# A two-block transformer kernel on one Trainium2 core: the order of attention pairs, the place of the neighbourhood bias, and three small reorderings

## The reference

```python
# first block
sh1, sc1, g1, sh2, sc2, g2 = split(silu(c) @ w_mod + b_mod)           # modulation
proj = modulate(rmsnorm(x), sh1, sc1) @ w_in                          # the same for 256 context tokens
q_m  = rmsnorm(q_lat) @ w_uq      ;  kn, v_m = rmsnorm(kv_lat) @ w_ukv
o_mla = dense_attention(q_m + rope, [k_ctx, k], [v_ctx, v])           # 8 latent heads, 512 keys
s = q_na @ k_na * scale + bias[h]; s = where(col_in, s, -1e30)        # 8 neighbourhood heads,
o_na = softmax([s, s_ctx]) @ [v, v_ctx]                               # 256 own + 256 context keys
x = x + g1 * (concat(o_mla, o_na) @ w_out)
x = x + g2 * hierarchical_moe(...)                                    # 16 experts, 2 per token in one group
# second block
u, v, q, k, v_b, f = rmsnorm(x) @ w_in2
x = x + concat(spatial_gating(u, v), forgetting_attention(q, k, v_b, f)) @ w_out2
x = x + conv_ffn(rmsnorm(x))
return rmsnorm(x)
```

## Time and profile before

| what | value |
|---|---|
| three runs | 744.06, 744.93, 747.24 us |
| median | 744.93 us |
| profiled execution | 743.41 us |
| its span in the trace | 741.6 us |
| granted TensorE clock, mean | 0.999 |
| TensorE / VectorE / ScalarE / GpSimd busy | 96% / 61% / 45% / 10% |
| moved from HBM | 197.9 MB, 268 GB/s over the span |

### The profile page before, as it was taken

How to read it: one execution, slowest core, us unless ns; L and a number is a source line. 1 busy time by engine, 2 the same in 40 slices (tenths; PEclk the granted TensorE clock), 3 DMA queues, 4 the chain that set the end, 5 groups by cost and what they waited for, 6 DMA issues and landing times.

```text
span 741.6 us, 10899 instructions
## 1 busy us (share of the span) xinstructions
PE 715.0 (96%) x4132; PEld 500.7 (68%) x4132; DVE 449.6 (61%) x776; ACT 332.3 (45%) x583; POOL 76.8 (10%) x83
## 2 busy tenths in 40 slices
PE   8899998999999999999999999999999999999997
PEld 3597887655785344353354357878889888888885
DVE  1597897799555211221221148969768999998443
ACT  2475233687524001110110137746547777776433
POOL 0000001043000000000000000040001344444000
PEclk9999999999999999999999999999999999999999
DMA  9995987625278999999999999006306446495101
GB/s 371 408 380 237 363 353 271 214 100 227 82 274 339 388 425 427 425 420 427 428 430 420 421 425 391 38 1 234 137 1 227 151 190 226 154 413 226 57 1 57
DMA packets 21258, 199.50 MB, mean 269 GB/s; under 512 B 2368, under 2 KB 2880, under 8 KB 4832
## 3 DMA queue, kind: packets, MB, share of 16 engines
q1 hardware_dynamic: 20304, 195.35, 65.5%
q0 software_dynamic: 624, 3.28, 1.3%
q10 hardware_dynamic: 288, 0.30, 0.1%
HBM read 197.86 MB, written 1.05 MB: 268 GB/s over the span
## 4 chain that ended last, share of the span: by engine, by line
PE 71%; DVE 13%; DMA 10%; ACT 3%; issue 1%; POOL 1%; SPq 0%; DVEq 0%; POOLq 0%; ACTq 0%
PE banks L1801 13%; PE banks L2074 10%; PE banks L2116 8%; PE banks L1339 6%; PE banks L1838 6%; DMA ring<-in_w_up 5%; PE banks L2078 5%; DVE ring L2308 3%; PE banks L1756 2%; DMA ring<-in_w_mod 2%; DMA ring<-in_w_col 2%; PE banks L1584 2%; PE banks L1585 2%; PE banks L1586 2%; DVE w_lo L2165 2%; DVE nmax L2360 2%
## 5 line engine op out<-in xcount | busy, mean ns | idle before, releaser
L2165 DVE TENSOR_TENSOR w_lo<-ring,w_hi 128x1024 fp32r<-128x1024 f32 (+1 forms) x123 | 147.5, 1204 | 48.1 <-ACT w_hi L1197 24.1
L1801 PE MATMUL banks<-ring,att 128*64 128x512 f32 x448 | 113.3, 593 | 2.4 <-DMA ring<-in_w_up 2.4
L2074 PE MATMUL banks<-h_both,w_hi 128*128 128x512 f32 x320 | 80.1, 392 | 0.0
L1801 PEld LDWEIGHTS banks<-ring,att 128*64 128x64 f32 x448 | 38.5, 137 | 59.7 <-issue 53.4
L888 ACT ACTIVATE w_hi<-ring 128x1024 fp32r<-128x1024 f32 x50 | 51.9, 1052 | 29.1 <-PE banks L1339 18.1
L2074 PEld LDWEIGHTS banks<-h_both,w_hi 128*128 128x128 f32 x320 | 57.6, 189 | 10.3
L2580 DVE TENSOR_TENSOR front<-front,banks 128x512 f32<-128x512 f32 x8 | 5.5, 688 | 95.4 <-PE banks L1801 95.4
L1192 ACT ACTIVATE w_hi<-ring 128x1024 fp32r<-128x1024 f32 x44 | 46.3, 1051 | 8.2 <-PE banks L2100 4.5
L2078 PEld LDWEIGHTS banks<-h_both,w_lo 128*128 128x128 f32 x320 | 43.6, 190 | 3.1
L2078 PE MATMUL banks<-h_both,w_lo 128*128 128x256 f32 x320 | 44.6, 282 | 0.0
L2553 DVE SCALAR_TENSOR_TENSOR ysb_lo<-banks,slot_w,ysb_hi 128x512 fp32r<-128x512 f32 x16 | 12.0, 751 | 52.2 <-ACT ysb_hi L1097 28.9
(11 more groups left out here) (398 smaller groups left out, 1524.0 us busy)
## 6 DMA issues: line engine op xcount, KB each, us to landing
ring<-in_w_up SPq DMA_DIRECT2D x21, 2048.0 KB, 9.1
ring<-in_w_down SPq DMA_DIRECT2D x9, 2048.0 KB, 12.5
ring<-in_w_in SPq DMA_DIRECT2D x8, 2048.0 KB, 18.7
ring<-in_w_gate SPq DMA_DIRECT2D x8, 2048.0 KB, 14.8
ring<-in_w_col SPq DMA_DIRECT2D x13, 1024.0 KB, 6.8
ring<-in_w_up SPq DMA_DIRECT2D x12, 1024.0 KB, 8.0
ring<-in_w_down SPq DMA_DIRECT2D x9, 1024.0 KB, 14.1
ring<-in_w_out SPq DMA_DIRECT2D x4, 2048.0 KB, 8.8
```

The source lines that it names most:

```text
L1801: last = nc.tensor.matmul(bank[2 + j][CAP * e:CAP * (e + 1), :], xs[:, k, at:at + CAP], gate_or_up(n + e, k, odd), start=(k == (4 if turne ...
L2074: nc.tensor.matmul(dst.rearrange("p (a t) -> p a t", a=2), granule(w_hi, j, g)[:, k, :], h2_both[:, :, k, :], start=(k == 0), stop=False, ...
L2165: return V.tensor_tensor(dst, src, high.bitcast(F32), ALU.subtract)
```

## The change

1. `PAIRS` runs over the head pair first and over latent and neighbourhood second: two latent steps, two neighbourhood steps, and so on. The output of step pair i goes to place `MIX_ORDER[i]`, and the projection sums over the places in that order.
2. The bias gets a place of its own: slot 3, once the query weights and the key weights there are used. GpSimd loads both halves and masks them ahead of the attention. The loads that used this slot (gate halves of expert 0) now stand behind the last product with the values, and two halves of the down weights, which go into `big` where the latent values are, wait for the seventh product instead of the fourth.
3. The splits of `w_out` move from steps 1, 3, 5, 7 to 1, 5, 8, 9.
4. The column sums 29, 30 and 31 move from behind product 21 (`ur 1`) to behind products 30, 32 and 34.
5. In the second block one part of `v 1` is made two steps earlier and two parts in the step between, and the low part of chunk 10 (for `q 1`) moves ahead of the residual products and the end of the layer norm.

```diff
-PAIRS = [(a, hp, q) for a in range(2) for hp in range(H // 2) for q in range(NT)]
+PAIRS = [(a, hp, q) for hp in range(H // 2) for a in range(2) for q in range(NT)]
+MIX_ORDER = [4 * a + hp for hp in range(H // 2) for a in range(2)]
...
-SPLIT_AT = (1, 3, 5, 7)
+SPLIT_AT = (1, 5, 8, 9)
...
-             19: (28,), 21: (29, 30, 31)}
+             19: (28,), 30: (29,), 32: (30,), 34: (31,)}
...
-        bias = arena[:, 0:4096].rearrange("p (h q n) -> p h q n", q=NT, n=T)
+        bias = ring[:, slot_of(L_UQ), :].rearrange("p (h q n) -> p h q n", q=NT, n=T)
...
-            sp.wait_ge(*through(last_in_slot(L_MOE)))
-            sp.wait_ge(lat_lo, 5)
-            for j in (0, 2):
-                expert_load(0, j)
             sp.wait_ge(prod_d, copied(PROD, at1("kn", 1))[1])
             gate_load(1, 0)
...
-            sp.wait_ge(ATT[0]["pv"], 4)
+            sp.wait_ge(ATT[0]["pv"], LAST // 2 - 1)
             for j in (8, 10):
                 spare_load(0, j)
             sp.wait_ge(ATT[0]["pv"], 8)
+            for j in (0, 2):
+                expert_load(0, j)
             spare_load(0, 11)
...
+            pool.wait_ge(kr_spread, 2)
+            pool.wait_ge(*through(L_UQ))
+            pool.wait_ge(lat_lo, 5)
+
+            def bias_half(half):
+                return ring[:, slot_of(L_UQ), 2048 * half:2048 * (half + 1)]
+
+            def bias_load(half):
+                pool.dma_start(bias_half(half), bias_d[:, 2048 * half:2048 * (half + 1)]).then_inc(in_pool, 16)
+
+            bias_load(0)
             for half in range(2):
-                pool.wait_ge(ATT[0]["scores"], 4 * (half + 1))
+                pool.wait_ge(in_pool, 16 * (half + 1))
                 if half == 0:
-                    pool.wait_ge(kr_spread, 2)
-                pool.dma_start(arena[:, 2048 * half:2048 * (half + 1)],
-                               bias_d[:, 2048 * half:2048 * (half + 1)]).then_inc(in_pool, 16)
-                pool.wait_ge(in_pool, 16 * (half + 1))
-                b = arena[:, 2048 * half:2048 * (half + 1)].rearrange("p (a n) -> p a n", n=GRID_W)
+                    bias_load(1)
+                b = bias_half(half).rearrange("p (a n) -> p a n", n=GRID_W)
...
             def pair_values(i):
-                v, hp = (vm, nav)[i // 4], i % 4
+                a, hp, _ = PAIRS[2 * i]
+                v = (vm, nav)[a]
...
-                    early_out(0, range(6))
+                    early_out(0, MIX_ORDER[:6])
...
-                    last = out_part(0, CHUNK1, OUT1, m, range((6, 6, 7)[m] if m < 3 else 0, KD))
+                    last = out_part(0, CHUNK1, OUT1, m, MIX_ORDER[(6, 6, 7)[m] if m < 3 else 0:])
...
             def beside_attention(s):
                 if s < 4:
-                    if s == 2:
+                    if s < 2:
+                        product2("v", 0, (2 * s, 2 * s + 1))
+                    if s == 1:
                         pe.wait_ge(y_made, KD)
-                    product2("v", s // 2, (2 * (s % 2), 2 * (s % 2) + 1))
+                    if s > 0:
+                        product2("v", 1, ((0,), (1, 2), (3,))[s - 1])
...
             def pair_outputs(i):
+                k = MIX_ORDER[i]
                 dve.wait_ge(A["pv"], i + 1)
-                high, src = mix_hi[0][:, i, :], bank[6][:, 0:T]
+                high, src = mix_hi[0][:, k, :], bank[6][:, 0:T]
                 link(V.tensor_copy(high, src))
-                low_part(mix_lo[0][:, i, :], src, high).then_inc(A["out"], 1)
+                low_part(mix_lo[0][:, k, :], src, high).then_inc(A["out"], 1)
...
             layer_norm()
-            for c in range(8, 10):
+            for c in range(8, 11):
                 chunk_to_lo(1, CHUNK2, c)
...
             layer_norm_end()
             forget()
-            chunk_to_lo(1, CHUNK2, 10)
             forget_end()
```

More of the change, by code:

```diff
@@ L1627, in _ @@
                     pe.wait_ge(A["out"], 6)
-                    early_out(0, range(6))
+                    early_out(0, MIX_ORDER[:6])
                 if s == 17:
-                    early_out(1, range(6))
+                    early_out(1, MIX_ORDER[:6])
                 if s == 18:
@@ L1633, in _ @@
                     pe.wait_ge(A["out"], 7)
-                    early_out(2, range(7))
+                    early_out(2, MIX_ORDER[:7])
             pe.wait_ge(A["out"], 8)
```

## The result

The changed kernel takes 748.60 us (median of 19 runs, 747.89 to 750.39), the kernel before 744.73 in the same comparison (19 runs): a ratio of 1.0051, 95% interval 1.0042 to 1.0060. It is 3.9 us slower, where the prediction said 2.5 us faster and a range that ended at 745.6. The profiled execution after has a span of 746.8 us (before 741.6).

What follows compares the result with a forecast made beforehand. TensorE (71% of the chain) and VectorE (13%) were taken to bound the kernel. −1.70 − 0.55 + 0.6 + 0 − 0.84 = −2.49 us, applied to the median 744.93, gave 742.4 us; range 739.8 to 745.6.

Steps and rivals of the forecast that it cites:

- Part 1, the sums: Ahead of the first attention: moving three column sums removes TensorE's wait before the key products, −1.70 us, bounds −1.7 and −0.7.
- the third sum just fits: Ahead of the first attention: column 31 runs to 137.25, with the first maximum due at 137.20 instead of 138.90.
- the second rival: "Time is moved, not removed": sums and masks meet and push the first maximum, alternation gives 0; 745.0 us, chance 0.20.
- the sentence on the Trainium skill: By the shared-port lock each sum could wait for a mask instruction: 1.4 in place of 0.6, total 743.2 us.
- Part 2, the alternation: First attention: alternating latent and neighbourhood pairs, with fewer early splits, gives −0.55 us, bounds −1.9 and +0.6.
- the right last wait: End of first attention: the seventh value products wait for the copy of pair 13, at 188.0 instead of 188.57.
- Four mixed pairs cost TensorE 12.9: First attention: four mixed pairs cost TensorE 12.9 us and VectorE 12.7, against 13.6 apart, at best 0.7 saved.
- Part 3, the masks: Start of first attention: the second mask stretches the first scaling pair, +0.6 us, bounds 0 and +1.4.
- Part 4, the transfers: Loads behind the first attention: the moved gate and down halves are absorbed, 0 us, bounds 0 and +4.9.
- Part 5, the second block: Second block: earlier low part and spread value products give −0.84 us, bounds −1.9 and +0.3.
- The copy of the rows: Second block: VectorE's copy at 479.26 now delays TensorE's `cq`, +0.25 in place of −0.82 us.
- The transfers as the slower rival: Moved 2.1 MB not absorbed between 199 and 222 us, experts' stream ends 4.9 us later: 749.0 us, chance 0.06.

Runs made afterwards that it cites:

- the sums back: The changed kernel with column sums 29, 30 and 31 together behind query tile 21 again, as in the kernel before: 744.53 us, ratio 1.0005.
- both loads ahead: The changed kernel with both bias halves issued one behind the other at the start, each on its own semaphore: 745.82 us.
- the next sum: The changed kernel with the load of the bias's second half issued behind a wait for the sum of tile 29: 745.05 us.
- the pause: The changed kernel with one pause in GpSimd's masks, the fifth waiting for the completion of the fourth: 746.67 us.
- the run begun in the middle: The changed kernel with the first-half masks begun by the end of the sum of tile 29, second bias half still landing: 745.36 us.

## Why the prediction was wrong

- **Part 1, the sums.** The mechanism was right and worth 1.97 us, not 1.70. The step "the third sum just fits" came true without masks (first maximum 136.84) and failed beside them. The prediction had the first mask from 129.9 to 136.3 and the three sums from 131.2 to 137.25, hence side by side, gave each sum its 1.2 us all the same, and priced only the first scaling. That term at nothing is what failed. The meeting went into the second rival, at 0.8 us for the sums and 0.8 for the masks, and into the sentence on the Trainium skill. It cost 6.25 us: 4.21 of waiting, 1.87 for scores at half clock, the rest in between. This term alone turns the sign.
- **The rule of the Trainium skill** (SBUF — State Buffer, "SBUF: two separate sides") named the right operations: held or slowed were sums and low parts with two SBUF inputs, and scalings from SBUF to SBUF, which are in the rule only if they run in its two-port mode (no run here shows the mode). Copies out of PSUM and maxima weren't (0.69 and 1.2 us beside the masks). The page has the loser wait for a whole instruction, so I took one mask of waiting for a sum, and 1.4 us in place of 0.6. With an issue right ahead the runs show eight masks; the measurement decides.
- **Part 2, the alternation,** −0.55 in the sum, measured 0. The walk was right up to the maxima (step 5 as before, steps 9 to 15 earlier by 1.1 to 1.3 us, where it had 1.6 to 1.7), and it named the right last wait. The term that was mis-sized is "Four mixed pairs cost TensorE 12.9", which has turns at 0.9 and latent scores at 1.72 everywhere. It measured 13.5, so TensorE's own queue keeps the seventh values where they were. Steps 2 and 3 lost nothing.
- **Part 3, the masks,** +0.6. In the changed kernel it shows as 0, because the attention is so late that the masks have ended before its first scalings. Once the sums aren't held, it is 1.5 to 4.2 us, above the bound of 1.4. The bound counted one pair of scalings, and where one pair is met (the sums back) the price is 1.5, with turns at half clock (1.97 us for 1.09) in it. In the other runs two pairs are met, in some also a low part, a wait for the bias and half clock.
- **Part 4, the transfers,** 0, and 0 it was: SyncE issues the moved gate halves at 204.50, behind the last product with the values, and TensorE's waits for `up` are 2.4 us in both.
- **Part 5, the second block,** −0.84, measured −0.7 in the profiled execution, where the clock didn't fall. The copy of the rows is late as foreseen (+0.29 at the product that waits for it, for +0.25). What the sum lacked is the clock behind the new wait, which takes 1.4 us in about half of the profiled executions.
- **The rivals.** "Time is moved, not removed" came nearest: its places are the right ones, its prices weren't. The transfers as the slower rival were the wrong mechanism.

**What stays open.** Every held sum or scaling stood beside masks that GpSimd began right behind its own issue, and so also with the load of that issue under way. The load alone doesn't hold (both loads ahead); an issue without a load under way no run shows. Nor does a run tell a wait of GpSimd from a mere delay behind the issue. In one run with the issue right ahead (the next sum, 745.05 us) VectorE already ran a sum when the masks came, the first mask gave way to it, and the next sum, which came into the middle of the run with the load still landing, was let in (1.55 us): who is first may decide too. So the issue is what the held cases share, not a shown cause. The hold ended at the pause, or at the last mask of a half, which raises a semaphore and is followed by a wait; which of the two frees VectorE, and why an issue has such an effect, no run here tells.

## What to carry to other kernels

Before you move work of VectorE, write down what GpSimd runs in the new place; if an operation with two SBUF inputs or a fast scaling is to lie beside a run of GpSimd, allow for a price of up to a whole run, not of one instruction, and look at the line's maximum in the trace, not at its median. In these runs two things freed VectorE: a wait in which GpSimd really stood between its own transfer issue and the run, or a pause inside the run; try them and measure. A wait that an edit adds to TensorE can cost more than its length, by the lower clock behind it. And before you trade idle time between engines, take the time from start to start of each instruction in the order in which it will stand: here 0.6 us on the turns and scores of four pairs used up nearly all of the 0.7 that was hoped for.

## What the hardware showed

- Eight masks of 0.70 us, run directly behind GpSimd's transfer issue, held a 1.22 us sum of VectorE for 6.80, 6.77 and 4.96 us, and a pair of scalings, normally 0.88, for 4.46. The same masks behind a real wait, or with a pause behind each, let VectorE in after one mask: sums took 1.2 to 2.0 us, and the mask beside them 1.6 to 1.8.
- A wait that was already met between issue and masks changed nothing (6.77 us).
- TensorE's granted clock fell to the lower level behind waits of 4.21, 4.43 and 2.69 us, and in 9 of 17 profiled executions behind a wait of only 0.72 us that followed one of 0.41; the work behind them then took 3.75 us for 1.88 and 5.54 for 4.04. The length of the wait alone doesn't tell: in the run begun in the middle TensorE waited 1.49 and 1.21 us and kept a clock of 1.00 in 142 to 150, in the run with both loads ahead it waited 1.27 and 0.66 and had 0.64 there.
- A group of eight turns took 0.87 us from start to start between two latent scores (before, 153.07) and 1.08 between two neighbourhood scores (before, 166.27).
